# First stage of a two-block sequence model: ScalarE's time-step exponentials moved by one block of evictions; the last block's transposes moved in among its own products, and its store waited for in the next stage

## What is computed

```python
def modulated_projection(h, norm_w, shift, scale, w_in):
    hm = rmsnorm(h, norm_w) * (1.0 + scale) + shift
    return hm @ w_in                      # 41 blocks of 128 columns
...
def ssd_bidir(xbc_raw, dt_raw, conv_w, conv_b, a_log, dt_bias, d_skip, h0):
    xbc = centred_dwconv(xbc_raw, conv_w, conv_b)
    ...
    dt = jax.nn.softplus(dt_raw.reshape(bsz, n, N_DIR, SSD_HEADS).astype(jnp.float32)
                         + dt_bias.astype(jnp.float32))
    a = -jnp.exp(a_log.astype(jnp.float32))
...
    z_pool = p[..., OFF_POOL_Z:OFF_SSD_Z]
    z_ssd = p[..., OFF_SSD_Z:OFF_XBC]
    y_pool = pool_mixer(u_pool, pool_w, pool_scale, grid) * jax.nn.silu(z_pool)
    gated = (y_ssd * jax.nn.silu(z_ssd)).reshape(bsz, n, SSD_GROUPS, W_SSD // SSD_GROUPS)
```

## Time and profile before

| | us |
|---|---|
| median of 3 runs | 3491.55 |
| lowest, highest | 3487.11, 3496.17 |
| the profiled execution | 3487.76 |
| its span, first to last instruction | 3486.1 |
| PE busy | 3263.6 (94%) |
| DVE busy | 1637.1 (47%) |
| ACT busy | 967.4 (28%) |

### The profile page before, as it was taken

One profiled execution on the slowest core, in us unless ns is written; L12 is line 12 of the kernel. 1 busy time (PEld: TensorE's weight loads), 2 busy tenths in 40 slices (PEclk: granted clock), 3 DMA queues, 4 the chain that ended last, 5 costly groups with the idle time before them and its releaser, 6 DMA issues. The chain is left out here.

```text
span 3486.1 us, 37796 instructions
## 1 busy us (share of the span) xinstructions
PE 3263.6 (94%) x15012; PEld 2561.4 (73%) x15012; DVE 1637.1 (47%) x1886; ACT 967.4 (28%) x1798; POOL 384.9 (11%) x246
## 2 busy tenths in 40 slices
PE   7899999997999979996999979999998799999898
PEld 7688888876887857774888867878877455555577
DVE  2754443466014237875444434323424455555365
ACT  2512221111211134541222222242323243433310
POOL 0100000000002125554000000000000201100012
PEclk9999999999999968887999989999999699999899
DMA  4222223342126345544333323222222421220233
GB/s 160 72 79 60 96 88 119 121 151 85 71 101 200 129 145 155 154 145 151 119 111 113 122 104 126 92 95 93 73 84 66 106 61 42 57 48 7 79 130 106
DMA packets 210926, 358.43 MB, mean 103 GB/s; under 512 B 22030, under 2 KB 143502, under 8 KB 202899
## 3 DMA queue, kind: packets, MB, share of 16 engines
q1 hardware_dynamic: 187030, 324.33, 28.9%
q10 hardware_dynamic: 16368, 26.36, 2.2%
q0 software_dynamic: 7392, 5.82, 0.8%
HBM read 234.57 MB, written 121.74 MB: 102 GB/s over the span
## 5 line engine op out<-in xcount | busy, mean ns | idle before, releaser
L636 PE MATMUL p_ps<-hmT_hi,p_w_hi 128*128 128x512 f32 x1312 | 524.4, 400 | 21.5 <-ACT p_work L356 15.9
L636 PE MATMUL p_ps<-hmT_hi,p_w_lo 128*128 128x512 f32 x1312 | 513.6, 391 | 0.0
L636 PE MATMUL p_ps<-hmT_lo,p_w_hi 128*128 128x512 f32 x1312 | 513.1, 391 | 0.0
L1751 PE MATMUL p_ps<-h2T_hi,p_w_hi 128*128 128x512 f32 x800 | 328.1, 410 | 19.3 <-DVE h2T_lo L1610 19.3
L1751 PE MATMUL p_ps<-h2T_hi,p_w_lo 128*128 128x512 f32 x800 | 316.1, 395 | 0.0
L1751 PE MATMUL p_ps<-h2T_lo,p_w_hi 128*128 128x512 f32 x800 | 315.8, 395 | 0.0
L636 PEld LDWEIGHTS p_ps<-hmT_hi,p_w_hi 128*128 128x128 f32 x1312 | 248.1, 189 | 75.5 <-issue 21.1
L636 PEld LDWEIGHTS p_ps<-hmT_hi,p_w_lo 128*128 128x128 f32 x1312 | 247.7, 189 | 53.1
L636 PEld LDWEIGHTS p_ps<-hmT_lo,p_w_hi 128*128 128x128 f32 x1312 | 248.2, 189 | 49.3
L1913 PE MATMUL t_psO<-t_prob,t_v 128*65 128x512 f32 (+3 forms) x640 | 261.0, 530 | 0.9 <-DVE t_out_turned L2023 0.2
L1970 ACT ACTIVATE t_prob<-t_psS 128x1024 f32<-128x1024 f32 (+1 forms) x160 | 150.2, 938 | 307.7 <-PE t_psS L1901 178.1
(11 more groups left out here) (370 smaller groups left out, 5873.4 us busy)
## 6 DMA issues: line engine op xcount, KB each, us to landing
p_w_raw<-in_w_in SPq DMA_DIRECT2D x66, 512.0 KB, 6.1
p_spare<-in_wada ACTq DMA_DIRECT2D x32, 512.0 KB, 5.5
p_spare<-scratch_xs_tok SPq DMA_DIRECT2D x19, 512.0 KB, 4.4
scratch_xs_tok<-p_work SPq DMA_DIRECT2D x8, 1152.0 KB, 6.1
p_work<-in_wada SPq DMA_DIRECT2D x16, 512.0 KB, 3.5
p_work<-in_x SPq DMA_DIRECT2D x16, 512.0 KB, 3.3
scratch_dT<-p_work SPq DMA_DIRECT2D x8, 1024.0 KB, 5.9
scratch_zpT<-p_work SPq DMA_DIRECT2D x8, 1024.0 KB, 4.0
```

What stands on the lines that cost most here:

```text
L636: mm = pe.matmul(PS[:, c, 0:width], wt[n][:, q, :], xx[:, q, cols], start=(q == 0 and j == 0), stop=(q == KT - 1 and j == 2))
L1751: mm = pe.matmul(ps[:, c, :], wt[n][:, q, :], xx[:, q, c * CH:(c + 1) * CH], start=(q == 0 and j == 0), stop=(q == KT - 1 and j == 2))
```

## The change

The first part moves four lines on ACT. In iteration `b == ZP` the two exponentials (with their waits) stood ahead of the evictions of block 25; they now stand behind them and behind `high(27)`. Nothing is added or removed.

The second part changes the last block. PE turns groups 0 and 1 of block 39 behind the first chunk of block 40, groups 2 and 3 behind the second, groups 0 and 1 of block 40 itself behind the third, group 2 behind the fourth, and group 3 after that. For block 40 each group now waits for its own eviction only. The turned block goes to the other half of `spare`. DVE's wait ahead of it is for the stored states, which lay there. The stage no longer waits for block 40's store. That store counts on a semaphore of its own, `last_z`, which lives on into `ssd`. There SP waits for it ahead of the first load of `w_out`, and DVE waits for it ahead of the two casts L954 and L955.

```diff
-        tok_of = lambda b: tok if b < NB - 1 else spare[:, 0:SEQ].rearrange("p (t c) -> p t c", c=P)
+        tok_of = lambda b: tok if b < NB - 1 else spare[:, SEQ:2 * SEQ].rearrange("p (t c) -> p t c", c=P)
...
-                        sp.dma_start(dst, tok_of(b)[:, 0:n, :]).then_inc(S["tok_out"], 16)
+                        sp.dma_start(dst, tok_of(b)[:, 0:n, :]).then_inc(S["tok_out"] if b < NB - 1 else s.last_z, 16)
...
                 store_tok(NB - 1)
-                sp.wait_ge(S["tok_out"], 16 * toks_before(NB))
+                sp.wait_ge(S["tok_out"], 16 * toks_before(NB - 1))
...
                     if 1 <= b <= DT:
                         silu(b - 1)
-                    if b == ZP:
-                        act.wait_ge(S["dt_in"], 64)
-                        act.activation(alog[:], alog[:], ACT.Exp).then_inc(S["exp"], 1)
-                        act.wait_ge(S["ask"], 1)
-                        act.activation(t0, t0, ACT.Exp).then_inc(S["exp"], 1)
...
                     if b + 2 < NB:
                         high(b + 2)
+                    if b == ZP:
+                        act.wait_ge(S["dt_in"], 64)
+                        act.activation(alog[:], alog[:], ACT.Exp).then_inc(S["exp"], 1)
+                        act.wait_ge(S["ask"], 1)
+                        act.activation(t0, t0, ACT.Exp).then_inc(S["exp"], 1)
...
-                v.wait_ge(S["summed"], len(STEPS))
+                v.wait_ge(h_out[0], 16 * 8)
+                v.wait_ge(h_out[1], 16 * 9)
                 read_groups(NB - 1, range(4))
...
                         if g == 0:
                             if b < DT:
                                 pe.wait_ge(S["act"], b + 1)
-                            else:
+                            elif b < NB - 1:
                                 pe.wait_ge(S["read"], chunks_before(b + 1))
+                        if b == NB - 1:
+                            pe.wait_ge(S["read"], chunks_before(b) + g + 1)
...
-                        elif b > ZS:
+                        elif ZS < b < NB - 1:
                             turn(b - 1, (c,))
+                        elif b == NB - 1:
+                            turn(*((b - 1, (0, 1)), (b - 1, (2, 3)), (b, (0, 1)), (b, (2,)))[c])
...
-                turn(NB - 1, range(4))
+                turn(NB - 1, (3,))
...
                         if c >= 2:
                             sp.wait_ge(S["w_lo"], c // 2)
+                        else:
+                            sp.wait_ge(s.last_z, 16)
                         sp.dma_start(piece[:], a["w_out"][:, c // 2, :]).then_inc(S["w_in"], 16)
...
                 v.wait_ge(S["masks_in"], 32)
+                v.wait_ge(s.last_z, 16)
                 v.tensor_copy(tri_r[:], tmp[:, 0:2 * P].rearrange("p (d l) -> p d l", l=P)).then_inc(S["const"], 1)
```

More of the change, by code:

```diff
@@ L2389, in program @@
         s.rstd_r = kit.sbuf(keep, "rstd_r", [P, LT])
+        s.last_z = nc.alloc_semaphore("last_z_stored")
         tables(nc, kit, a, s)
```

## The result

| | before | changed |
|---|---|---|
| median, us | 3489.33 (6 runs) | 3465.54 (6 runs) |
| lowest, highest | 3484.89, 3496.17 | 3458.6, 3472.86 |
| ratio, 95% interval | | 0.9931 (0.9913 to 0.9950) |
| the profiled execution, its span | 3487.76, 3486.1 | 3461.25, 3459.5 |

The kernel became faster by 23.8 us. The question is where the further 9 us come from: from the change, or from chance.

What follows compares the result with a forecast made beforehand. PE, busy 94% of the span, was taken as the bound, gaining only from stops or half clock. Exponentials 9.5 us plus last block 5.3 us made 14.8 us, so 3491.55 became 3476.8 us, range 3468 to 3486.

Steps and rivals of the forecast that it cites:

- The first stop: PE's 15.9 us stop behind block 25, in the first stage: PE restarts at 828.35, 13.8 us earlier than 842.13.
- The clock's price: Half clock on PE behind its 4.3 us wait ahead of the cumulative sums: costs 1.7 us of the gain there.
- the new stop: PE waits ahead of the cumulative sums for DVE's time steps, from 850.2 to 854.5: 4.3 us.
- The wait for `last_z`: DVE's added wait ahead of casts L954 and L955, and SP's: cost nothing; DVE's decides only from 3.2 us of delay.
- The second part: Last block and stage boundary: store 1.3 us earlier, `ssd` starts 6.1 us earlier, PE's start 4.5 to 6.1, taken as 5.3.
- the burst of loads: Loads at the start of `ssd`, overlapping the last store by 1.6 us: delayed by 0 to 1.6 us.
- a term near 6.1: Upper end at PE's start in `ssd`, if the store holds back SP's own loads and POOL's constants only by their share.
- The sum to the first L987: Total gain up to the second stage's start: 9.5 us from the exponentials plus 5.3 us from the last block, 14.8 us.
- the first term: Exponentials moved behind block 25's evictions: sums 11.2 us earlier, less 1.7 for half clock, 9.5 us; ends 8.5 and 11.2.
- the term for the second stage's clock: `ssd`, 354 us at mean clock 0.81: a fall to 0.778 loses the gain, 0.756 makes it 10.5 us slower; chance 0.05.
- the fourth rival: Clock goes the other way, or both bounds fall well: 11.2 + 6.1 = 17.3 and 3 us of clock, 3471 us; chance 0.09.
- The base: Starting time of the kernel before, the median shown, 3491.55 us, from which the 14.8 us were subtracted.

## Why the prediction was wrong, point by point

**The first stop: right.** Forecast was a restart at 828.35, a second stop until 854.5 and sums 11.2 us earlier. Measured were 828.65, 854.90 and 10.8 us in the first profile; from the gate columns to the sums it is 166.8 to 166.9 us in five profiles, 178.1 to 179.3 before, 11.8 us in the mean. The list names ACT's eviction as the releaser. By the times it is DVE's low half, as forecast: it ended at 828.59, 0.06 us ahead of the restart, and the eviction, begun at 827.55, some 0.4 us earlier.

**The clock's price: the right size, in one course of two.** I took 1.7 us behind the new stop, from the earlier trace rows, and said that a price behind the short stop would be hidden. Two of the five profiles of the changed kernel (sums behind a stop of 2.5 and 2.6 us) took the hidden course. The other three (4.0 to 4.2 us) took the one that I had reckoned with, at 1.5 us, with the same start of the sums. So the price was 0.9 us in the mean. I also held that nothing changes behind the sums, and overlooked that PE has another stop of 1.8 to 2.2 us at 1088 to 1101 us, in both kernels. Behind it the half clock came in four of five profiles of the changed kernel and in two of five of before, at some 1.6 us each. From the gate columns to ACT's last eviction the five profiles gave 9.1 us, and with the 1.25 us of transposes added back 10.4, for the 9.5 forecast.

**The wait for `last_z`: right.** The casts on DVE waited for the masks' load, as before. What released PE's first products varies between `cT`, the casts and `seg_l`, which lie close together.

**The second part: right, a little too large.** The store's 1.3 us came true (2.7 against the last product, less 1.25), and the first DMA 2.2 us behind it where I had 2.0. The three groups of transposes took 1.25 us, not 1.4. At the first L987, 6.0 us were gained against the last product, so 4.7 in all. I had 5.3. The missing 0.6 us lie toward the lower end that I named, the burst of loads beside the store: from the first DMA to the first L987 11.9 to 12.4 us became 13.1 to 13.4. What I had argued from the Trainium skill, "DMA: Bandwidth & Descriptors", section "Queues, rings and completion order", for a term near 6.1 did not come true. POOL's 8 KB constant was indeed not held back (6.3 us to landing, before 7.4). But the first L987 is released by another load of POOL, and that took 1.2 us longer. PE's first products, some 4 us ahead of it, were released in three of the five profiles by `cT` from SP's queue and in two by DVE's casts, where before it was the constant each time.

**The sum to the first L987: 14.8 forecast, 15.1 measured** as the mean of five profiles. That it fits to 0.3 us is luck in part: the first term was 0.9 too small and the second 0.6 too large.

**The step that failed** is the term for the second stage's clock, and with it the width of the range. In the fourth rival I allowed that clock 3 us in the kernel's favour, and I gave the median half of three runs' spread. The stretch of `ssd` alone moved by 7 us among profiles of before and by 13 us among those of the changed kernel, and the second projection by 4. The row that I had the earlier trace rows shows a mean clock of 0.81 with a busy PE. I priced a fall of that clock (0.778 and 0.756), but not a rise of like size: to 0.85 it would have been 354 x 0.81 / 0.85 = 337 us by my own formula, 17 us. The measured 0.85 gave 9 to 12, so the formula also overprices: not all of that stage goes with the clock. I did not carry the range through either. The fourth rival's 3471.25 less the 4.5 us of spread is 3466.7, not 3468, and even that lies above the measured 3465.54.

The base failed too. From my 3476.8 to the measured 3465.54 it is 11.3 us. Of these 4.8 are the three-run median that I started from, 3491.55 where 60 runs of before have 3486.8; 3.0 are the first six runs of the changed kernel, which lie that far under the median of all 27; and 3.5 are gain beyond my sum, of which it is open how much follows from the change. The path through the two stops needed no correction beyond its sizes; on the terms that I had, the range should have reached down by some 10 us.

## What to carry to other kernels

When an instruction waits at the head of an in-order queue for something that the work behind it doesn't need, move it behind that work; then sum what PE meets next, for here a 15.9 us stop became 2.1 and 2.5 to 4.2 us, because DVE's chain was not moved. A stage boundary need not wait for its last store if the next stage's first users of that memory wait: here it gave 4.4 us at the first DMA, of which 3 were left where PE started, since the store then shared the DMA engines with the loads. And where a stage runs between two clock levels, take several profiles before a difference in an unedited stage is put down to an edit.

## What the runs showed of the hardware

A stop of 2.1 us behind 22 us of steady products was followed by some 3.4 us at half clock in two of five executions of the same kernel and by none in the others, and in 5 of the 11 profiles of all kernels with the exponentials moved. Stops of 4.0 to 4.2 us were followed by it in all three of that kernel's profiles that had one. Equal code at the same place was granted 0.82 to 0.85 of the clock over 350 us, and its length differed by up to 13 us. A PE that entered the second stage at full clock was back at half after 5 us of matmuls broken by one wait of 1.5 us. And loads issued 2.2 us behind a 1 MB store slowed it from 5.2 to 5.8 us, and a 64 KB load beside it from 2.7 to 5.5 us.
